# A two-block transformer kernel on one core: four orders changed, and the keys of differential attention prepared as whole tiles, with 64-row matmuls for their low parts

## The chip, the cores and the metric

The kernel is one program on one core of a Trainium2 chip. Five engines take part: TensorE (PE, with its weight loads shown apart as PEld), VectorE (DVE), ScalarE (ACT), GpSimd (POOL) and SyncE (SP), which only issues transfers. The metric is device time in microseconds, median of three executions.

## The reference, cut to what matters

A sequence of 512 tokens of width 1024 in float32 goes through two transformer blocks. The first has sliding-window attention with sinks beside retention, and a convolutional GELU feed-forward. The second has two SwiGLU feed-forwards around a mix of differential attention and a three-branch sparse attention. The part that the larger edit touches is differential attention, with 8 heads, each with two components of 64:

```python
q = apply_rope(q, cos, sin); k = apply_rope(k, cos, sin)
s = jnp.einsum('bqhcd,bkhcd->bhcqk', qb, k).astype(jnp.float32) * scale
s = jnp.where(kpos[None, :] <= qpos[:, None], s, NEG_INF)
p = jax.nn.softmax(s, axis=-1)
a = p[:, :, 0] - lam * p[:, :, 1]
return jnp.einsum('bhqk,bkhe->bqhe', a.astype(v.dtype), v)
```

The other edits lie at the very start (RMS norm of `x`), in the sliding-window attention with its rotary embedding of the retention's queries and keys, and where the compressed branch of the sparse attention hands over to the other two branches.

## The kernel before, in words

**Numbers in two parts.** Every float32 operand of a product is split into a high part (a cast to fp32r) and a low part (the value less its high part), and a product is three matmuls: high by high, high by low, low by high. ScalarE casts, VectorE subtracts. Weights come in chunks of 128x1024 through six slots (`raw`, `Wh`, `Wl`); SyncE reloads a slot once the chunk in it has been used.

**Order.** Nothing schedules the work: each engine runs a program written out by hand, with semaphores between them. What stands behind a waiting instruction on its engine waits too. Softmax tiles are interleaved with steps of matrix products that need nothing new, to fill TensorE's time.

**The start.** SyncE issues `X` tile 0, then the gain `gpre0` (one row broadcast to 128 partitions), `X` tile 1, a weight chunk and so on. `normed(0, 0)` on VectorE needs both `X` tile 0 and the gain. TensorE transposes (`turn_tile`, line 792) and starts the first product (`first_half`, line 739).

**The local attention.** For each of 8 heads, TensorE turns the probabilities (line 963) and multiplies them by the values (lines 985, 986). VectorE does per head `local_low` (`ALl`, 2156), `local_gate` of the next head (`PL`, 2151), `local_max`, `local_sum`, and one `rope_turned` (lines 1943, 2127, 2129), a rotary step of a retention tile, and mostly a weight split (1842).

**Differential attention.** 32 score tiles, `t = 0..31`, four per head; tile `t` has `(t % 4 + 1) * 128` keys and two components `m`, each with its own bank. The queries stand in `Qst` as a stack: for component `m` the 64 partitions of that component hold the high part and the other 64 the low part. `Kh` holds the key's high part in both halves, so that one matmul over 128 rows gives two of the three products (line 854). `Kl` holds the low part in one half and zeros in the other; the matmul of line 855 gives the third product. Line 856 adds the causal mask in bfloat16. GpSimd prepares a head in `qk_low`: it casts the key in two halves (line 574), subtracts in two halves (579) and makes the queries' low halves (585); `v_low` makes the low part of the values `Vst` (592). Each head's other half of `Kh` comes by two transfers of 64 partitions by SyncE (line 490), which waits for the casts (`k_hi`) and stands in the same queue as the weight loads. On TensorE, `values(4h)` waits for the `v_low` of head `h`, and `scores(4h)` for `qk_low` and for the transfers. GpSimd begins head `h` once `high(4(h-2)+2)` has run on ScalarE, which tells it that head `h-2` no longer needs the buffers.

The order of TensorE in the loop is `values(t-2)`, `scores(t+2)`, `turn(t)`, one step of another product.

**The last attention stage.** Before its loop, TensorE does two gate chunks of 8 steps, and `cmp_turn(1)` (line 1159), which needs `cmp_weigh(1)` of VectorE; `unit_turn(0)` (line 1203) then needs the banks that `cmp_low(1)` (`CAl`, line 2370) frees.

Of the kernel before, what the change touches and what calls it, by code (L numbers as in the profile page):

```python
# [7 lines left out]
F32 = mybir.dt.float32  # L8
F32R = mybir.dt.float32r
# [5 lines left out]
P = 128  # L15
# [85 lines left out]
def program(nc, t, out, stop=None):  # L101
# [9 lines left out]
    with ExitStack() as ctx:  # L111
# [111 lines left out]
        Kh = at("Kh", 40, [P, 2, 2, SEQ], F32R)  # L223
        Kl = at("Kl", 80, [P, 2, 2, SEQ], F32R)
        swp_d = at("swp_d", 64, [P, 2, SEQ])
# [101 lines left out]
        st_hi = sem("st_hi")  # L327
        st_zero = sem("st_zero")
        st_lo = sem("st_lo")
        k_twin = sem("k_twin")  # L330
        k_hi = sem("k_hi")
# [55 lines left out]
        def qk_parts(head):  # L387

            return (0, 5)[head] if head < 2 else 5 * head - 1

        def v_parts(head):

            return min(9 + 5 * head, 40) if head else 5

        def q_parts(head):

            return (0, 3)[head] if head < 2 else 3 * head - 1

        def v_casts(head):

            return min(5 + 3 * head, 24) if head else 3

# [44 lines left out]
        def _(sp):  # L447
            w = t["w_all"]
            g = t["g_pre"][0]
            for tt in range(TT):  # L450
                sp.dma_start(X[:, tt, :], t["x"][tt * P:(tt + 1) * P, :]).then_inc(in_x[tt], 16)
                if tt == 0:
                    sp.dma_start(gpre0[:], g.rearrange("(a n) -> a n", a=1).broadcast_to((P, D))).then_inc(in_gain0, 16)
                if tt:
                    sp.dma_start(raw[:, tt - 1, :], w[tt - 1]).then_inc(w_raw[tt - 1], 16)
# [11 lines left out]
            def swaps(m):  # L467
# [15 lines left out]
                if m in TWIN_AT and on("da"):  # L483
                    for head in TWIN_AT[m]:
                        u = head % 2
                        sp.wait_ge(k_hi, 2 * head + 2)
                        for comp in range(2):
                            own = slice(HD * comp, HD * comp + HD)
                            other = slice(HD * (1 - comp), HD * (1 - comp) + HD)
                            sp.dma_start(Kh[other, u, comp, :].bitcast(F32), Kh[own, u, comp, :].bitcast(F32)).then_inc(k_twin, 16)  # L490
                if m == CHUNK0["nsf"] + 3 and on("nsf"):
# [28 lines left out]
        def _(pl):  # L520
# [43 lines left out]
            if on("da"):  # L564
                def qk_low(it, head):

                    u = head % 2
                    k = qkd[:, span(it, 2, 8 + head, 1), :].rearrange("p a n -> p (a n)")
                    if head >= 2:
                        pl.wait_ge(at_hi, 4 * (head - 2) + 3)  # L570
                    for m in range(2):
                        own = slice(HD * m, HD * m + HD)
                        pool.drain()
                        pool.tensor_copy(Kh[own, u, m, :], k[own, :])
                        pool.drain().then_inc(k_hi, 1)
# [20 lines left out]
                pl.wait_ge(roped, 8 + 16)  # L596
                for m in range(2):
                    other = slice(HD * (1 - m), HD * (1 - m) + HD)
                    for u in range(2):
                        last = pool.memset(Kl[other, u, m, :].bitcast(F32), 0.0)  # L600
                last.then_inc(st_zero, 1)
                qk_low(0, 0)
                v_low(0, 0)
                qk_low(0, 1)
                for head in range(2, 8):
# [87 lines left out]
        def _(pe):  # L693
# [149 lines left out]
            def scores(t):  # L843
                i, u, b2 = t % 4, t // 4 % 2, 2 * (t % 2)
                w = width(t)
                q = slice(i * P, (i + 1) * P)
                if i == 0:
                    pe.wait_ge(st_lo, qk_parts(t // 4) + 4)
                    pe.wait_ge(k_twin, 32 * (t // 4) + 32)
                for m in range(2):  # L850
                    b = b2 + m
                    bank_free("da", b, t // 2)
                    dst = ps[b][:, 0:w]
                    tensor.matmul(dst, Qst[:, u, m, q], Kh[:, u, m, 0:w], start=True, stop=False)
                    tensor.matmul(dst, Qst[:, u, m, q], Kl[:, u, m, 0:w], start=False, stop=False)
                    tensor.matmul(ps[b][:, w - P:w], identb[:], causal, start=False, stop=True).then_inc(full[b], 1)
# [245 lines left out]
            if on("da"):  # L1102
                pe.wait_ge(st_zero, 1)
                attention()
# [76 lines left out]
            if on("nsa"):  # L1181
# [80 lines left out]
                gate_steps(1, 0, 4)  # L1262
                gate_steps(1, 4, 8)
                cmp_turn(1)
                for s in range(32):
                    unit_turn(s)
# [49 lines left out]
        def _(ac):  # L1316
# [183 lines left out]
            def nsf_out(c):  # L1500
                chunk_done("nsf", c)
                if c >= 2:
                    ac.wait_ge(st_lo, qk_parts((4, 7)[c - 2]) + 4)
                dst = kcv[:, c, :] if c < 2 else kraw[:, c - 2, :]
                scalar.copy(dst, ps[7][:]).then_inc(free[7], 1)

            def attention():
                exps(0)
                v_high(0)
                exps(1)  # L1510
                qk_high(1)
                for t in range(TOTAL):
# [165 lines left out]
            if on("vda"):  # L1678
                for c in range(7):
                    split(CHUNK0["vda"] + c + LEAD)  # L1680
                    if c == 3 and on("da"):
                        ac.wait_ge(roped, 24)
                        qk_high(0)
                for tt in range(TT):
                    bank_done("vda", tt, 1)
# [70 lines left out]
            if on("nsa"):  # L1756
# [25 lines left out]
                split(CHUNK0["nsa"] + LEAD)  # L1782
                split(CHUNK0["nsa"] + 1 + LEAD)
                unit_exps(1)
                cmp_high(1)
                for s in range(32):
# [48 lines left out]
        def _(ve):  # L1835
# [287 lines left out]
            if on("local"):  # L2123
# [53 lines left out]
                for h in range(8):  # L2177
# [7 lines left out]
                    if h:  # L2185
                        local_sum(h - 1)
                    if h < 7:
                        rope_turned(h + 1)
                    if h < 4:
                        split(CHUNK0["rope_r"] + h + 3 + LEAD)  # L2190
                    if h == 5:
                        split(CHUNK0["rope_r"] + 7 + LEAD)
                local_sum(7)
            if on("vg"):
                splits_t("vg", 5)
# [206 lines left out]
            if on("nsa"):  # L2402
# [38 lines left out]
                cmp_weigh(1)  # L2441
                split(CHUNK0["nsa"] + LEAD)
                split(CHUNK0["nsa"] + 1 + LEAD)
                gate_out(1)
                cmp_low(1)
                for s in range(32):
# [206 lines left out]
```

## Time and profile before

| what | us |
|---|---|
| median of 3 executions (2008.1 to 2018.64) | 2008.75 |
| the profiled execution's own time | 2007.84 |
| its span in the trace | 2006.0 |
| TensorE busy | 1976.0 |
| VectorE busy | 1048.3 |
| ScalarE busy | 810.8 |
| GpSimd busy | 283.2 |

Busy time is the union of an engine's instructions in the span. A matmul's duration includes its way through the array, so that matmuls in a row overlap, and the distance from one start to the next is shorter than the duration.

### The profile page before, as it was taken

What the parts mean: (1) busy time and instruction counts of PE and PEld (TensorE: products, weight loads), DVE (VectorE), ACT (ScalarE), POOL (GpSimd) and SP (SyncE); (2) the same over time, 40 slices, a digit from 0 to 9 for tenths busy, and PEclk for the clock granted to TensorE, in tenths of its full rate; (3) what the DMA queues carried; (4) which work ended last, traced back from release to release, by engine and by line L of the source; (5) the groups of instructions that cost most, each with busy time, mean ns of one, the idle gap of its engine ahead of it and who ended that gap; (6) DMA issues with size and microseconds to landing.
All of it is one profiled execution on the core that took longest, in us unless ns stands there. A gap on an engine that the chain in (4) does not pass through costs nothing.

```text
span 2006.0 us, 25493 instructions
## 1 busy us (share of the span) xinstructions
PE 1976.0 (99%) x10112; PEld 1667.8 (83%) x10112; DVE 1048.3 (52%) x1607; ACT 810.8 (40%) x1474; POOL 283.2 (14%) x290
## 2 busy tenths in 40 slices
PE   7999999999999999999999999999999999999998
PEld 7888888888888888888988788888888888888887
DVE  5766665555353322334563868877775543222333
ACT  5542443333343222233423864466663332222332
POOL 1001000000000000000002734377751000000000
PEclk9999999999999999999999999999999999999999
DMA  6331333333323333332453135221126423333332
GB/s 211 105 95 53 116 106 99 100 95 95 96 94 105 95 96 101 97 95 74 137 153 104 43 115 176 79 64 49 48 64 210 124 67 114 95 99 101 95 95 74
DMA packets 60261, 202.22 MB, mean 101 GB/s; under 512 B 8336, under 2 KB 8368, under 8 KB 59760
## 3 DMA queue, kind: packets, MB, share of 16 engines
q1 hardware_dynamic: 56080, 185.10, 29.9%
q0 software_dynamic: 4064, 15.49, 2.4%
q8 instruction: 81, 1.33, 0.3%
q14 instruction: 36, 0.29, 0.0%
HBM read 181.16 MB, written 8.39 MB: 94 GB/s over the span
## 4 chain that ended last, share of the span: by engine, by line
PE 68%; issue 25%; DVE 3%; ACT 1%; DMA 1%; DVEq 1%; POOLq 1%; POOL 0%; SPq 0%; ACTq 0%
PE ps L700 19%; PE ps L702 19%; PE ps L701 19%; PE ps L1203 2%; PE ps L1192 1%; PE ps L1241 1%; PE ps L1240 1%; PE ps L1193 1%; PE ps L1119 1%; DVE XN L1882 1%; ACT XN L1356 0%; PE ps L1048 0%; PE ps L1194 0%; PE ps L1037 0%; PE ps L792 0%
## 5 line engine op out<-in xcount | busy, mean ns | idle before, releaser
L1842 DVE TENSOR_TENSOR Wl<-raw,Wh 128x1024 fp32r<-128x1024 f32 x307 | 378.5, 1236 | 694.1 <-ACT Wh L1323 692.7
L700 PE MATMUL ps<-HTh,Wh 128*128 128x512 f32 (+1 forms) x1712 | 643.8, 376 | 1.9 <-DVE HTl L2475 1.0
L702 PE MATMUL ps<-HTh,Wl 128*128 128x512 f32 (+1 forms) x1712 | 636.9, 372 | 0.0
L701 PE MATMUL ps<-HTl,Wh 128*128 128x512 f32 (+1 forms) x1712 | 636.6, 372 | 0.0
L1323 ACT CAST Wh<-raw 128x1024 fp32r<-128x1024 f32 x307 | 321.7, 1051 | 741.3 <-DMA raw<-in_w_all 741.3
L700 PEld LDWEIGHTS ps<-HTh,Wh 128*128 128x128 f32 x1712 | 323.1, 189 | 55.9 <-issue 1.8
L702 PEld LDWEIGHTS ps<-HTh,Wl 128*128 128x128 f32 x1712 | 322.4, 188 | 56.3
L701 PEld LDWEIGHTS ps<-HTl,Wh 128*128 128x128 f32 x1712 | 322.8, 189 | 53.2
L700 PE MATMUL ps<-Wh,Yh 128*128 128x512 f32 x528 | 205.8, 390 | 0.0
L702 PE MATMUL ps<-Wh,Yl 128*128 128x512 f32 x528 | 205.5, 389 | 0.0
L701 PE MATMUL ps<-Wl,Yh 128*128 128x512 f32 x528 | 205.4, 389 | 0.0
L656 POOL TENSOR_SCALAR PU<-PU,ugg 128x512 f32<-128x512 f32 (+3 forms) x128 | 139.2, 1103 | 79.3 <-DVE ugg L2414 79.3
L702 PEld LDWEIGHTS ps<-Wh,Yl 128*128 128x128 f32 x528 | 99.1, 188 | 20.7
L700 PEld LDWEIGHTS ps<-Wh,Yh 128*128 128x128 f32 x528 | 99.1, 188 | 20.5
L701 PEld LDWEIGHTS ps<-Wl,Yh 128*128 128x128 f32 x528 | 99.1, 188 | 20.3
L700 PE MATMUL ps<-Wh,HTh 128*128 128x512 f32 (+1 forms) x288 | 110.7, 384 | 0.0
L702 PE MATMUL ps<-Wh,HTl 128*128 128x512 f32 (+1 forms) x288 | 109.4, 380 | 0.0
L701 PE MATMUL ps<-Wl,HTh 128*128 128x512 f32 (+1 forms) x288 | 109.3, 380 | 0.0
L1761 ACT ACTIVATE PU<-ps,umx 128x512 f32<-128x512 f32 (+3 forms) x128 | 65.8, 527 | 53.6 <-DVE umx L2406 53.6
L600 POOL MEMSET Kl<- 64x512 f32 x4 | 2.0, 522 | 453.5 <-DVE qkd L1951 453.5
L702 PEld LDWEIGHTS ps<-Wh,HTl 128*128 128x128 f32 x288 | 54.1, 188 | 10.2
L701 PEld LDWEIGHTS ps<-Wl,HTh 128*128 128x128 f32 x288 | 54.1, 188 | 9.7
(288 smaller groups left out, 2388.0 us busy)
## 6 DMA issues: line engine op xcount, KB each, us to landing
raw<-in_w_all SPq DMA_DIRECT2D x307, 512.0 KB, 3.5
swp_d<-qkd SPq DMA_DIRECT2D x64, 64.0 KB, 2.9
g_dram<-gst SPq DMA_DIRECT2D x16, 256.0 KB, 3.9
ring<-g_dram POOLq DMA_DIRECT2D x16, 256.0 KB, 3.6
X<-in_x SPq DMA_DIRECT2D x4, 512.0 KB, 7.5
swp_r<-qkr SPq DMA_DIRECT2D x16, 128.0 KB, 3.6
gpre<-in_g_pre POOLq DMA_DIRECT2D x4, 512.0 KB, 4.0
Kh<-Kh SPq DMA_DIRECT2D x16, 128.0 KB, 2.3
```

Of the source, the lines that this page charges most:

```text
L656: last = pool.tensor_scalar(p, p, ugg[:, s % 2, i:i + 1], None, ALU.mult)
L700: tensor.matmul(dst, a_hi, b_hi, start=start, stop=False)
L701: tensor.matmul(dst, a_hi, b_lo, start=False, stop=False)
L702: return tensor.matmul(dst, a_lo, b_hi, start=False, stop=stop)
L1119: last = tensor.matmul(ps[kv][:, ht * 64:ht * 64 + 62], cw[:, j, ht * P:(ht + 1) * P], cA[:, kv, j, :], start=j == 0, stop=j == 15)
L1192: tensor.matmul(ps[b][:, o:o + w], q, ksh[:, m, g, 0:w], start=True, stop=False)
L1193: tensor.matmul(ps[b][:, o:o + w], q, ksl[:, m, g, 0:w], start=False, stop=False)
L1203: return tensor.transpose(dst, p[:, a:a + P], ident[:])
L1240: tensor.matmul(ps[b][:, k * P:], v, AUh[:, o:o + w], start=False, stop=False)
L1323: scalar.copy(Wh[:, s, :], raw[:, s, :]).then_inc(w_hi, 1)
L1761: last = scalar.activation(PU[:, (s + 1) % 2, SCORE_AT[i]:SCORE_AT[i] + w], ps[b][:, o:o + w], ACT.Exp, bias=umx[:, s % 2, i:i + 1], accum ...
L1842: vector.tensor_tensor(Wl[:, s, :], raw[:, s, :], Wh[:, s, :], ALU.subtract).then_inc(w_lo, 1)
```

## The change

Five places are changed.

1. SyncE issues `gpre0` behind `X` tile 1 instead of behind `X` tile 0.
2. In the local attention, `rope_turned(6)` and `rope_turned(7)` leave VectorE's iterations 5 and 6 and come behind the loop.
3. Differential attention: `Kl` becomes `Kp`, with the key's high part of both components in plane 0 and the low part in plane 1. GpSimd casts the key in one 128-partition instruction and subtracts in one; the zeroing of `Kl` and its semaphore go. `Kh` is filled by four transfers of 64 partitions per head, each from `Kp`, where two copied within `Kh`. The matmul for the low part of the keys reads only the 64 partitions of its component, from `Qst` and from `Kp`: it is issued with a tile of 64 rows by 128 columns, at row 0 for component 0 and at row 64 for component 1, between matmuls of 128 by 128.
4. The preparation of head 1 moves: GpSimd does `qk_low(0, 1)` ahead of `v_low(0, 0)`, and ScalarE casts head 1's queries within the `vda` product, not after `exps(1)`.
5. At the start of the last attention stage, `cmp_turn(1)` moves ahead of three of the eight steps of the second gate chunk on TensorE, `cmp_high(1)` ahead of `unit_exps(1)` on ScalarE, and `cmp_low(1)` ahead of one weight split and a copy on VectorE.

```diff
             for tt in range(TT):
                 sp.dma_start(X[:, tt, :], t["x"][tt * P:(tt + 1) * P, :]).then_inc(in_x[tt], 16)
-                if tt == 0:
+                if tt == 1:
                     sp.dma_start(gpre0[:], g.rearrange("(a n) -> a n", a=1).broadcast_to((P, D))).then_inc(in_gain0, 16)
...
                         u = head % 2
-                        sp.wait_ge(k_hi, 2 * head + 2)
+                        sp.wait_ge(k_hi, head + 1)
                         for comp in range(2):
                             own = slice(HD * comp, HD * comp + HD)
-                            other = slice(HD * (1 - comp), HD * (1 - comp) + HD)
-                            sp.dma_start(Kh[other, u, comp, :].bitcast(F32), Kh[own, u, comp, :].bitcast(F32)).then_inc(k_twin, 16)
+                            for half in (slice(0, HD), slice(HD, P)):
+                                sp.dma_start(Kh[half, u, comp, :].bitcast(F32), Kp[own, u, 0, :].bitcast(F32)).then_inc(k_twin[u], 16)
...
-                    for m in range(2):
-                        own = slice(HD * m, HD * m + HD)
-                        pool.drain()
-                        pool.tensor_copy(Kh[own, u, m, :], k[own, :])
-                        pool.drain().then_inc(k_hi, 1)
-                    for m in range(2):
-                        own = slice(HD * m, HD * m + HD)
-                        pool.drain()
-                        pool.tensor_tensor(Kl[own, u, m, :], k[own, :], Kh[own, u, m, :], ALU.subtract).then_inc(st_lo, 1)
+                    pool.drain()
+                    pool.tensor_copy(Kp[:, u, 0, :], k)
+                    pool.drain().then_inc(k_hi, 1)
+                    pool.tensor_tensor(Kp[:, u, 1, :], k, Kp[:, u, 0, :], ALU.subtract).then_inc(st_lo, 1)
...
                 if i == 0:
-                    pe.wait_ge(st_lo, qk_parts(t // 4) + 4)
-                    pe.wait_ge(k_twin, 32 * (t // 4) + 32)
+                    pe.wait_ge(st_lo, qk_parts(t // 4) + 3)
+                    pe.wait_ge(k_twin[u], 64 * (t // 8) + 64)
...
                     tensor.matmul(dst, Qst[:, u, m, q], Kh[:, u, m, 0:w], start=True, stop=False)
-                    tensor.matmul(dst, Qst[:, u, m, q], Kl[:, u, m, 0:w], start=False, stop=False)
+                    own = slice(HD * m, HD * m + HD)
+                    tensor.matmul(dst, Qst[own, u, m, q], Kp[own, u, 1, 0:w], start=False, stop=False)
...
-                    if h < 7:
+                    if h < 5:
                         rope_turned(h + 1)
```

The order on three engines, before and now. First GpSimd at the start of differential attention, before; `Kh`, `Kl` and `Qst` are the parts named above, `Vst` the values' low part of a head.

```order
L600 MEMSET Kl 64x512 x4
L574 CAST Kh<-qkd 64x512 x2
L579 TENSOR_TENSOR Kl<-qkd,Kh 64x512 x2
L585 TENSOR_TENSOR Qst<-qkd,Qst 64x512 x2
L592 TENSOR_TENSOR Vst<-vd,Vst 128x512
L574 CAST Kh<-qkd 64x512 x2
L579 TENSOR_TENSOR Kl<-qkd,Kh 64x512 x2
L585 TENSOR_TENSOR Qst<-qkd,Qst 64x512 x2
L574 CAST Kh<-qkd 64x512 x2
```

Now:

```order
L571 CAST Kp<-qkd 128x512
L573 TENSOR_TENSOR Kp<-qkd,Kp 128x512
L579 TENSOR_TENSOR Qst<-qkd,Qst 64x512 x2
L571 CAST Kp<-qkd 128x512
L573 TENSOR_TENSOR Kp<-qkd,Kp 128x512
L579 TENSOR_TENSOR Qst<-qkd,Qst 64x512 x2
L586 TENSOR_TENSOR Vst<-vd,Vst 128x512
L571 CAST Kp<-qkd 128x512
L573 TENSOR_TENSOR Kp<-qkd,Kp 128x512
```

The four memsets are gone, one 128-partition instruction stands where two of 64 did for the cast and for the subtraction, and head 0's values (`Vst`) now stand behind head 1's keys and queries.

VectorE at the end of the local attention, from head 4's `local_sum` (`CATT`), before; `swp_r` and `qkr` are the rotary step, `Wl` a weight split.

```order
L2163 TENSOR_TENSOR CATT<-ps,llo 64x512
L1943 TENSOR_TENSOR swp_r<-swp_r,sin 128x512
L2127 TENSOR_TENSOR qkr<-qkr,cos 128x512
L2129 TENSOR_TENSOR qkr<-qkr,swp_r 128x512
L1842 TENSOR_TENSOR Wl<-raw,Wh 128x1024
L2156 TENSOR_TENSOR ALl<-ps,ALh 128x512
L2158 TENSOR_TENSOR ALl<-ps,ALh 128x384
L2145 TENSOR_TENSOR lsum<-lsum,lsk 128x4
L2147 RECIPROCAL lsum<-lsum 128x4
L2151 TENSOR_SCALAR PL<-PL,lsum 128x128
L2151 TENSOR_SCALAR PL<-PL,lsum 128x256 x3
L2163 TENSOR_TENSOR CATT<-ps,llo 64x512
```

Now:

```order
L2154 TENSOR_TENSOR CATT<-ps,llo 64x512
L1833 TENSOR_TENSOR Wl<-raw,Wh 128x1024
L2147 TENSOR_TENSOR ALl<-ps,ALh 128x512
L2149 TENSOR_TENSOR ALl<-ps,ALh 128x384
L2136 TENSOR_TENSOR lsum<-lsum,lsk 128x4
L2138 RECIPROCAL lsum<-lsum 128x4
L2142 TENSOR_SCALAR PL<-PL,lsum 128x128
L2142 TENSOR_SCALAR PL<-PL,lsum 128x256 x3
L2154 TENSOR_TENSOR CATT<-ps,llo 64x512
L2147 TENSOR_TENSOR ALl<-ps,ALh 128x512
L2149 TENSOR_TENSOR ALl<-ps,ALh 128x384
L2154 TENSOR_TENSOR CATT<-ps,llo 64x512
```

The rotary step no longer stands ahead of the weight split and of head 6's `ALl`, nor that of the next iteration ahead of head 7's; both come behind the last row shown.

VectorE at the start of the last attention stage, from `cmp_weigh(1)`'s last instruction on, before; `CAl` is `cmp_low(1)`, `gst` the gate chunk's copy.

```order
L2365 TENSOR_TENSOR CS_123<-CS_123,cst 128x32x31
L1842 TENSOR_TENSOR Wl<-raw,Wh 128x1024 x2
L2433 COPY gst_132<-ps 128x512
L2370 TENSOR_TENSOR CAl<-ps,CAh 128x512 x2
L2412 RECIPROCAL ugg<-usum 128x4
```

Now:

```order
L2358 TENSOR_TENSOR CS_123<-CS_123,cst 128x32x31
L1833 TENSOR_TENSOR Wl<-raw,Wh 128x1024
L2363 TENSOR_TENSOR CAl<-ps,CAh 128x512 x2
L1833 TENSOR_TENSOR Wl<-raw,Wh 128x1024
L2426 COPY gst_132<-ps 128x512
L2405 RECIPROCAL ugg<-usum 128x4
```

`CAl` now comes behind one split instead of behind two and a copy.

## Rows read from the trace of the kernel before

**Rows 1.** page, part 1: busy us (share of span) and instructions of each engine.
```profile
PE 1976.0 (99%) x10112; PEld 1667.8 (83%) x10112; DVE 1048.3 (52%) x1607; ACT 810.8 (40%) x1474; POOL 283.2 (14%) x290
```

**Rows 2.** stretches: us, busy of PE, PEld, DVE, ACT, POOL, granted clock, DMA share, GB/s.
```profile
1090.00:1195.00 105.00, 97.59 (x670) 81.69 (x670) 83.82 (x200) 77.89 (x226) 59.60 (x52) 1.00 0.26 77
```

**Rows 3.** whom TensorE waited for: us in total, times, longest us.
```profile
PE ps L792 <- DVE XN L1882: 10.1, 4, 7.8
PE ps L700 <- issue: 3.4, 6, 1.0
PE ps L864 <- DVE Pb L2048: 2.2, 5, 0.6
PE ps L854 <- POOL Qst L585: 1.2, 1, 1.2
...
PE ps L985 <- DVE ALl L2156: 1.0, 1, 1.0
...
PE ps L963 <- DVE PL L2151: 0.6, 1, 0.6
```

**Rows 4.** timeline of the start: start us, us, engine, line, op [idle before <-releaser].
```profile
6.41 1.28 DVE L1882 SCALAR_TENSOR_TENSOR XN<-X,rstd,gpre 128x1024 f32<-128x1024 f32 x1 [0.32 <-DMA gpre<-in_g_pre]
...
8.39 1.06 ACT L1356 ACTIVATE XN<-X 128x1024 f32<-128x1024 f32 x1 [2.50 <-DMA X<-in_x]
...
11.52 1.97 PE L792 MATMUL ps<-ident,XN 128*128 128x128 f32 x8 [1.74 <-DVE XN L1882]
```

**Rows 5.** timeline of VectorE at the end of the local attention.
```profile
120.69 0.69 DVE L1943 TENSOR_TENSOR swp_r<-swp_r,sin 128x512 f32<-128x512 f32 x1
...
122.67 1.22 DVE L1842 TENSOR_TENSOR Wl<-raw,Wh 128x1024 fp32r<-128x1024 f32 x1
```

**Rows 6.** timeline of GpSimd, one head of the differential attention.
```profile
1119.85 1.03 POOL L574 CAST Kh<-qkd 64x512 fp32r<-64x512 f32 x1 [0.23 <-issue]
...
1122.57 1.28 POOL L579 TENSOR_TENSOR Kl<-qkd,Kh 64x512 fp32r<-64x512 f32 x1 [0.16 <-issue]
...
1126.90 1.26 POOL L592 TENSOR_TENSOR Vst<-vd,Vst 128x512 fp32r<-128x512 f32 x1 [0.16 <-issue]
```

**Rows 7.** timeline of TensorE at the same place.
```profile
1128.26 0.30 PE L700 MATMUL ps<-Vst,ATdh 128*128 128x128 f32 x1 [1.03 <-issue]
```

**Rows 8.** timeline of VectorE at the start of the last attention stage.
```profile
1281.18 1.19 DVE L2365 TENSOR_TENSOR CS<-CS,cst 128x992 f32<-128x992 f32 x1
...
1286.19 1.29 DVE L2370 TENSOR_TENSOR CAl<-ps,CAh 128x512 fp32r<-128x512 f32 x2 [0.37 <-ACT CAh L1733]
```

**Rows 9.** timeline of TensorE there: second gate chunk, cmp_turn(1), unit_turn(0).
```profile
1279.36 0.47 PE L700 MATMUL ps<-HTh,Wh 128*128 128x512 f32 x1 [0.92 <-DVE gst L2433]
...
1284.93 1.04 PE L1159 MATMUL ps<-ident,CS 128*128 128x128 f32 x8
1287.02 1.38 PE L1203 MATMUL ps<-ident,PU 128*128 128x128 f32 x10 [1.06 <-DVE CAl L2370]
```

**Rows 10.** TensorE groups by shape, 1090 to 1230 us: busy us, mean ns of one.
```profile
L854 PE MATMUL ps<-Kh,Qst 128*128 128x256 f32 x16 | 5.6, 350 | 0.0
...
L855 PE MATMUL ps<-Kl,Qst 128*128 128x256 f32 x16 | 4.5, 280 | 0.0
```

**Rows 11.** timeline of one score tile: weight load, matmul, and the matmul behind it.
```profile
1131.28 0.19 PEld L855 LDWEIGHTS ps<-Kl,Qst 128*128 128x128 f32 x1
...
1131.39 0.28 PE L855 MATMUL ps<-Kl,Qst 128*128 128x256 f32 x1
...
1131.52 0.23 PE L856 MATMUL ps<-band,identb 128*128 128x128 bf16 x1
```

**Rows 12.** timeline of ScalarE, value cast of the same head.
```profile
1125.15 0.62 ACT L1547 CAST Vst<-vd 128x512 fp32r<-128x512 f32 x1
```

**Rows 13.** page, part 6: transfers, count, KB each, us from issue to landing.
```profile
Kh<-Kh SPq DMA_DIRECT2D x16, 128.0 KB, 2.3
```

**Rows 14.** timeline of SyncE: issue of one head's transfers.
```profile
1077.47 1.14 SPq L490 DMA_DIRECT2D Kh<-Kh  x2
```

More of the change, by code:

```diff
@@ L223, in program @@
         Kh = at("Kh", 40, [P, 2, 2, SEQ], F32R)
-        Kl = at("Kl", 80, [P, 2, 2, SEQ], F32R)
+        Kp = at("Kp", 80, [P, 2, 2, SEQ], F32R)
         swp_d = at("swp_d", 64, [P, 2, SEQ])
@@ L327, in program @@
         st_hi = sem("st_hi")
-        st_zero = sem("st_zero")
         st_lo = sem("st_lo")
-        k_twin = sem("k_twin")
+        k_twin = [sem(f"k_twin{u}") for u in range(2)]
         k_hi = sem("k_hi")
@@ L387, in qk_parts @@
         def qk_parts(head):
-            return (0, 5)[head] if head < 2 else 5 * head - 1
+            return (0, 3)[head] if head < 2 else 4 * head - 1
         def v_parts(head):
-            return min(9 + 5 * head, 40) if head else 5
+            return min(7 + 4 * head, 32)
         def q_parts(head):
-            return (0, 3)[head] if head < 2 else 3 * head - 1
+            return (0, 2)[head] if head < 2 else 3 * head - 1
         def v_casts(head):
-            return min(5 + 3 * head, 24) if head else 3
+            return min(5 + 3 * head, 24)
         def nsf_ends(t):
@@ L596, in _ @@
                 pl.wait_ge(roped, 8 + 16)
[L597 to L601, printed above, removed]
                 qk_low(0, 0)
+                qk_low(0, 1)
                 v_low(0, 0)
-                qk_low(0, 1)
                 for head in range(2, 8):
@@ L1102, in _ @@
             if on("da"):
-                pe.wait_ge(st_zero, 1)
                 attention()
@@ L1262, in _ @@
                 gate_steps(1, 0, 4)
-                gate_steps(1, 4, 8)
+                gate_steps(1, 4, 5)
                 cmp_turn(1)
+                gate_steps(1, 5, 8)
                 for s in range(32):
@@ L1502, in nsf_out @@
                 if c >= 2:
-                    ac.wait_ge(st_lo, qk_parts((4, 7)[c - 2]) + 4)
+                    ac.wait_ge(st_lo, qk_parts((4, 7)[c - 2]) + 3)
                 dst = kcv[:, c, :] if c < 2 else kraw[:, c - 2, :]
@@ L1510, in attention @@
                 exps(1)
-                qk_high(1)
                 for t in range(TOTAL):
@@ L1683, in _ @@
                         qk_high(0)
+                    if c == 4 and on("da"):
+                        qk_high(1)
                 for tt in range(TT):
@@ L1783, in _ @@
                 split(CHUNK0["nsa"] + 1 + LEAD)
+                cmp_high(1)
                 unit_exps(1)
-                cmp_high(1)
                 for s in range(32):
@@ L2192, in _ @@
                         split(CHUNK0["rope_r"] + 7 + LEAD)
+                rope_turned(6)
                 local_sum(7)
+                rope_turned(7)
             if on("vg"):
@@ L2442, in _ @@
                 split(CHUNK0["nsa"] + LEAD)
+                cmp_low(1)
                 split(CHUNK0["nsa"] + 1 + LEAD)
                 gate_out(1)
-                cmp_low(1)
                 for s in range(32):
```

## The prediction

> **What bounds the kernel now.** I read the page's busy times first: TensorE is busy for 1976.0 of 2006.0 us [rows 1]. An edit is therefore worth what it takes out of TensorE's 30 us of idle time, less what it adds to TensorE's own work; VectorE at 52% and ScalarE at 40% are idle for half of the span on average, so time on them counts only where TensorE waits for it. Next the list of TensorE's waits [rows 3], which says where the 30 us are: 10.1 at the transposes of the norms, nearly all at the start, where nothing can run yet; 3.4 in six pieces put down to "issue"; 2.2 in five pieces for `Pb`; 1.2 for `Qst`; 1.0 and 0.6 in the local attention. Then the busy time by stretches [rows 2]: of the 105 us from 1090 to 1195, which hold differential attention, TensorE is busy for 97.59, so 7.4 us are idle there. The granted clock is 1.00, the upper level of 2.4 GHz. Last I read timelines of those places, for what ended each wait.
>
> **Edit 1, the gain behind `X` tile 1: 0.** VectorE's first norm began at 6.41, released by the gain; ScalarE's squares of tile 1 began at 8.39, released by `X` [rows 4]. The two transfers are of one size and trade places, so I put the gain at 8.4 and tile 1 at 6.4. Then both norms run back to back, 8.4 + 2 x 1.28 = 11.0, but the first transposes start at 9.8 instead of 7.8 and hold TensorE for about 2 us, as the second set did (1.97, from 11.52) [rows 4]. The second set starts at 9.8 + 1.95 = 11.7 against 11.52. That is 0.2 later, with earlier squares and a first weight cast that may give it back. I take 0, with bounds of 0.6 either way.
>
> **Edit 2, two rotary steps out of the local loop: 1.6 gained.** A step holds VectorE from 120.69 to 122.67, 1.98 us [rows 5]. TensorE then waits 1.0 for `ALl` of head 6 and 0.6 for `PL` of head 7, both behind that step in VectorE's order [rows 3]. With 1.98 gone and 1.6 needed, both waits go, 0.4 to spare; head 7's `ALl` comes 4 us earlier. The steps aren't lost: they run behind the loop, where VectorE has only weight splits, and the retention, which needs them, stands behind the whole `vg` product.
>
> **Edits 3 and 4, differential attention outside the matmuls: 4.0 gained.** The 1.2 us for `Qst` is head 1's preparation, which queues behind head 0's values. It moves ahead of them, and so do ScalarE's casts for it; that wait goes. The six waits of 3.4 us called "issue" I read as waits for GpSimd: `v_low` ran from 1126.90 for 1.26, to 1128.16 [rows 6], and TensorE's first value product of that head started at 1128.26 after 1.03 idle [rows 7]. The other five stand in the same distance to the other heads' `v_low`. Per head the edit takes one cast with its gap (1.03 + 0.23) and one subtraction with its gap (1.28 + 0.16) off GpSimd ahead of `v_low`: 2.7 us [rows 6]. What is late next is ScalarE's cast of the values, 1125.15 + 0.62 = 1125.77 [rows 12], so `v_low` can end at 1125.77 + 1.26 = 1127.03, and TensorE, which was ready at 1128.26 - 1.03 = 1127.23, no longer waits, with 0.1 to spare in this head, the tightest. The five waits for `Pb` (2.2) stay, since they hang on scores that move with TensorE. The sum is 1.2 + 3.4 = 4.6; with so little to spare I take off 0.6. Four transfers replace two: they are 4 x 128 KB per head, each 2.3 us to land [rows 13]. SyncE takes 1.14 to issue two [rows 14], so 2.3 for four, and the last lands 4.6 behind the cast. TensorE's scores of the head stand behind the value product that waits for `v_low`, and `v_low` is the fourth GpSimd instruction of 1.28 behind the cast: 5.1 without gaps. The transfers stay hidden by 0.5 or more. Without that cover, at most the added issue time of 1.14 would show in each of 8 heads, 9 us. The weight loads behind them in SyncE's queue move back by the same 1.14, and TensorE has no wait for a weight in this list [rows 3]. The 4 memsets stood before GpSimd had anything urgent: 0.
>
> **Edit 3, the 64-row matmuls: unknown, taken at 0.** 64 matmuls (32 tiles, two components) change from 128 rows to 64, each between matmuls of 128 rows: 128 changes of shape. No matmul of this trace has 64 rows. From below: a matmul of 256 keys takes 280 ns here [rows 10] with a start-to-start distance of 1131.52 - 1131.39 = 0.13 [rows 11]; the distance goes with the columns, which stay, so I see no gain, and the lower end is 0. The nearest row on a change between neighbours is one of element type: `Kh`'s matmul comes behind the bfloat16 mask or another product and takes 350 ns, `Kl`'s of the same shape behind `Kh`'s takes 280 [rows 10], 70 ns more. At 0.07 for each of 128 changes that is 9 us. From above: at each change the array would empty (0.28 - 0.13 = 0.15) and the weights would be loaded with nothing beside them (0.19) [rows 11]: 0.34 x 128 = 44 us. I take 0: the row of 350 ns also carries the first start after a change of tile and queries, and half of the new changes fall on the very boundary with the mask that pays this already.
>
> The page "TensorE: Matmul & The Clock Gate" of the Trainium skill, section "Why this matters for your kernels", says that one matmul of few rows takes the same time as one of 128; by that the term is 0. No run here shows it yet.
>
> **Edit 5, entry to the last stage: 1.1 gained.** TensorE's second gate chunk ran 1279.36 to 1284.93, 0.70 a step; `cmp_turn(1)` followed, and `unit_turn(0)` began at 1287.02 after 1.06 idle [rows 9], for `CAl`, which ran from 1286.19 [rows 8]. `cmp_turn(1)` moves three steps, 2.1 us, ahead, to 1279.36 + 5 x 0.70 = 1282.86. What it needs was ready at 1281.18 + 1.19 = 1282.37 [rows 8], so it doesn't wait. `CAl` can start near 1284.1 and take 1.29, to 1285.4, before 1285.96, when TensorE is there. `gate_out(1)` moves behind, and only a later gate chunk needs it. 1.1 gained.
>
> **The sum.** 0 + 1.6 + 4.0 + 1.1 = 6.7. The profiled execution took 2007.84, so 2001.1; the median stands 0.9 above that execution, so 2002.0. I add 0.5 for waits that appear in place of those removed: 2002.5.
>
> **The rivals.**
> A, the forecast, 2002.5, by itself 2000 to 2006. For it: every wait it counts has its row and its releaser.
> B, the shape change costs like a change of type. 9 us, less 6.7: 2008.75 - 6.2 + 9 = 2011.5. For it, the 70 ns above; against it, that the columns set the distance elsewhere.
> C, slower: the array empties at each change. At 0.15 the sum is 128 x 0.15 = 19.2, so 2008.75 - 6.2 + 19.2 = 2021.8; with exposed weight loads, 44 us, 2046. It decides from 6.2 / 128 = 48 ns per change upwards, and by over 0.5% from 16.2 / 128 = 127 ns. Against it: no row shows such a thing; for it: 128 places.
> By the page "TensorEngine Tiling (Array Packing)", section "Key Properties", of the Trainium skill, changing the tiling mode drains the TensorE. That is this rival; no row of before can show whether it holds at such a boundary or what it costs.
> D, the differential attention edits don't do what they say: the "issue" waits are not GpSimd's, or ScalarE and VectorE (busy for 83.82 of 105 us there [rows 2]) take their place. Then 1.2 of 4.0 stays, and the time is 2005.3.
>
> **Chances.** A 0.56, B 0.20, C 0.12, D 0.12. Within 0.5% (10 us, about what a measurement of this kernel can tell from no change) is 1998.7 to 2018.8. Faster by more would need more than the 3.4 + 2.2 + 1.2 + 1.0 + 0.6 + 1.1 = 9.5 us of waits behind the start that rows 3 and rows 9 name, so something from the start as well: 0.03, out of A. Slower by more is C and the top of B: 0.13. The rest, 0.84, is no change. The range for 8 in 10 takes in A, B and D: 1999.5 to 2014.
>
> **What would show it.** In the trace after: the waits for `ALl` and `PL` near 124 and 126 are absent; the list has no "issue" waits at the value products and none for `Qst`; `unit_turn(0)` follows without idle time. The start-to-start distance between `Kh`'s matmul, the 64-row one and the mask tells the rest: unchanged (0.13 from the low part's matmul to the mask for 256 keys) means A, longer by 0.05 to 0.1 each B, by 0.15 or more C. A time above 2012 says that the shape change isn't free.

## The result, and the profile after

| | before | after |
|---|---|---|
| median of 12 executions each, us | 2007.62 (2007.0 to 2018.64) | 2021.88 (2012.74 to 2028.9) |
| own time of the profiled execution | 2007.84 | 2023.69 |
| its span | 2006.0 | 2021.8 |

The change makes the kernel slower, by under one per cent: the ratio is 1.0045, 95% interval 1.0028 to 1.0062. The executions of both kernels fall in two groups, about 10 us apart, so the difference depends on what is compared: 14.3 us between the medians, 11.1 between the means, 5.4 between the medians of the two lower groups. Of before, 10 lie at 2007.0 to 2008.8 and 2 at 2018.5 and 2018.6; of after, 3 lie at 2012.74 to 2013.22, 8 at 2021.2 to 2023.7 and one at 2028.9. The two groups are part of the story below, since the change moves most executions from one to the other.

The span grew by 15.8 us. The page's part 1 of after, against [rows 1]: TensorE is busy 21.5 us longer, with the same number of instructions (the stretch at the lower clock, told of below, is part of it), and GpSimd 17 us less.

```profile
PE 1997.5 (99%) x10112; PEld 1680.5 (83%) x10112; DVE 1047.6 (52%) x1607; ACT 810.4 (40%) x1474; POOL 266.1 (13%) x270
```

TensorE's waits, in the form of [rows 3]: engine, tile, line, releaser, then us in total, times, longest.

```profile
PE ps L781 <- DVE XN L1873: 9.9, 3, 9.5
PE ps L1108 <- DMA w2v<-in_w2v: 3.0, 1, 3.0
...
PE ps L1192 <- POOL PU L645: 0.9, 1, 0.9
...
PE ps L854 <- DVE Pb L2039: 0.3, 1, 0.3
```

The waits for `Qst`, for `ALl` and `PL`, for `CAl` and the six "issue" waits are gone, as forecast, and `Pb` (2.2 before) has shrunk to 0.3. The wait of 0.9 for `PU` is new. The one for `w2v`, weights of the sparse attention that the change doesn't touch, has grown to 3.0; the last line of before's list is

```profile
PE ps L1119 <- DMA w2v<-in_w2v: 0.3, 1, 0.3
```

The stretches, in the columns of [rows 2]; the second holds the end of differential attention and the compressed keys of the sparse attention, the third a part of it.

```profile
1090.00:1195.00 105.00, 104.44 (x616) 79.16 (x615) 81.63 (x197) 74.23 (x219) 41.93 (x34) 1.00 0.29 76
1195.00:1262.00 67.00, 64.02 (x370) 58.84 (x370) 39.49 (x50) 24.89 (x40) 20.84 (x24) 0.87 0.48 161
1225.00:1245.00 20.00, 18.76 (x80) 17.78 (x81) 14.30 (x15) 4.39 (x4) 7.49 (x8) 0.57 0.27 74
```

In the first stretch TensorE is busy for 104.44 of 105 us (97.59 before) and yet does less: differential attention, from the first `Kh` matmul to the last value product, took 104.83 us before and takes 113.09. Something makes its matmuls longer. The groups by shape, to be read against [rows 10] (busy us, mean ns of one, idle):

```profile
L845 PE MATMUL ps<-Kp,Qst 64*128 64x256 f32 x16 | 6.1, 380 | 0.0
L843 PE MATMUL ps<-Kh,Qst 128*128 128x256 f32 x16 | 5.6, 350 | 0.0
```

`Kh`'s matmul still takes 350 ns. The low part's, of the same 256 keys, takes 380 where it took 280. The distances from start to start say it more exactly. In the trace before I took a tile of 256 keys [rows 11]; this is one of 384 keys of before, and below it the same of after. Columns: start, us, engine, line, tile.

```profile
1134.28 0.39 PE L854 MATMUL ps<-Kh,Qst 128*128 128x384 f32 x1
1134.51 0.34 PE L855 MATMUL ps<-Kl,Qst 128*128 128x384 f32 x1
1134.68 0.23 PE L856 MATMUL ps<-band,identb 128*128 128x128 bf16 x1
```

```profile
1134.20 0.39 PE L843 MATMUL ps<-Kh,Qst 128*128 128x384 f32 x1
1134.52 0.44 PE L845 MATMUL ps<-Kp,Qst 64*128 64x384 f32 x1
1134.89 0.23 PE L846 MATMUL ps<-band,identb 128*128 128x128 bf16 x1
```

From `Kh`'s matmul to the mask it was 0.40, now 0.69. Over all 64 such places the sum of these distances is 24.17 us before and 41.47 after: 17.3 us for 128 changes of shape, 0.135 each. The two components pay alike. The weight loads show what is lost. The loads of the same places in after:

```profile
1134.14 0.19 PEld L843 LDWEIGHTS ps<-Kh,Qst 128*128 128x128 f32 x1
1134.52 0.18 PEld L845 LDWEIGHTS ps<-Kp,Qst 64*128 64x128 f32 x1 [0.18 <-issue]
1134.89 0.10 PEld L846 LDWEIGHTS ps<-band,identb 128*128 128x128 bf16 x1 [0.18 <-issue]
```

In [rows 11] the low part's load starts at 1131.28 and its matmul at 1131.39: 0.11 of the load ran beside the matmul ahead. Now load and matmul are both put at 1134.52, 0.19 after the load ahead of it has ended (the bracket in the row says 0.18 idle). The median of this lead over the 64 places is 144 ns before and 2 ns after. The load of 64 rows no longer begins beside a matmul of 128 rows. It takes 0.18; the distance from `Kh` to the mask grew by 0.27 per tile and component, a load and 0.09 more. The mask's load led by nothing before either (4 ns, then and now), but the low part's matmul ahead of it now holds its own load: from the low part to the mask the mean distance grew from 163 to 342 ns, from `Kh` to the low part from 214 to 306. So 0.18 of the 0.27 stand at the second boundary and 0.09 at the first.

The second thing stands behind differential attention. TensorE at the first matmul of the compressed keys, before and after:

```profile
1218.30 7.36 PE L1119 MATMUL ps<-cA,cw1k 128*128 128x62 f32 x64 [0.25 <-DMA w2v<-in_w2v]
```

```profile
1226.24 2.18 PE L1108 MATMUL ps<-cA,cw1k 128*128 128x62 f32 x9 [2.98 <-DMA w2v<-in_w2v]
```

The issue of the two transfers concerned, before and after (`w2v` by GpSimd, `cw1v`, 2 MB, by SyncE):

```profile
1212.10 0.53 POOL L526 DMA_DIRECT2D w2v<-in_w2v  x1
...
1212.25 0.33 SPq L471 DMA_DIRECT2D cw1v<-in_cw  x1
```

```profile
1216.15 0.33 SPq L470 DMA_DIRECT2D cw1v<-in_cw  x1
...
1217.30 0.54 POOL L525 DMA_DIRECT2D w2v<-in_w2v  x1
```

Before, GpSimd issued `w2v` 0.15 ahead of SyncE's `cw1v`; after, 1.15 behind it. The list of transfers (count, KB each, us from issue to landing) has GpSimd's two small ones, before and after; `w2k` is issued 0.55 ahead of `w2v`:

```profile
w2k<-in_w2k POOLq DMA_DIRECT2D x1, 128.0 KB, 2.7
w2v<-in_w2v POOLq DMA_DIRECT2D x1, 64.0 KB, 6.2
```

```profile
w2k<-in_w2k POOLq DMA_DIRECT2D x1, 128.0 KB, 7.4
w2v<-in_w2v POOLq DMA_DIRECT2D x1, 64.0 KB, 8.9
```

TensorE reaches the place 5.2 us later than before and `w2v` is issued 5.2 later, so the longer landing, 8.9 against 6.2, is the whole of the added wait: 2.98 against 0.25. Its granted clock falls too: 0.57 on average from 1225 to 1245 (the table of stretches), and in the trace's record it is at the lower of its two levels, 1.2 GHz, for 17.07 us, from 1225.76 on, 0.5 before the wait ends. At half speed that is up to 8.5 us lost beside the wait of 3.0; the 64 matmuls of the compressed keys' first product alone take 13.9 us where they took 7.4. The clock's row of the page's part 2 (40 slices of the span, tenths of full speed) has its one 8 there, and no other dip:

```profile
PEclk9999999999999999999999998999999999999999
```

### The profile page after: what moved, and what is told of

Its sections match the earlier page's. It is cut to its first block, busy times and chain, and to the rows that moved or that the text cites. A ratio compares the mean times of both kernels' runs of the same rounds, so it can differ in the third digit from the quotient of the medians.

```text
span 2021.8 us, 25456 instructions
## 1 busy us (share of the span) xinstructions
PE 1997.5 (99%) x10112; PEld 1680.5 (83%) x10112; DVE 1047.6 (52%) x1607; ACT 810.4 (40%) x1474; POOL 266.1 (13%) x270
## 4 chain that ended last, share of the span: by engine, by line
PE 94%; DVE 2%; DMA 1%; ACT 1%; issue 1%; POOL 1%; DVEq 0%; POOLq 0%; SPq 0%; ACTq 0%
PE ps L689 27%; PE ps L691 27%; PE ps L690 27%; PE ps L1192 2%; PE ps L1108 1%; PE ps L1181 1%; PE ps L845 1%; PE ps L1230 1%; PE ps L1229 1%; PE ps L1182 1%; PE ps L781 1%; POOL PU L645 1%; PE ps L843 1%; DVE XN L1873 1%; PE ps L846 0%
## 5 line engine op out<-in xcount | busy, mean ns | idle before, releaser
L571 POOL CAST Kp<-qkd 128x512 fp32r<-128x512 f32 x8 | 6.7, 840 | 483.9 <-issue 455.4
```

## The experiments

Each was timed in three rounds, with runs of before on the same chip. e1 to e4 share 31 runs of before (median 2008.57; 20 at 2006.8 to 2010.8, 11 at 2015.5 to 2019.7), e5 to e7 and e4b share 28 (median 2008.26; 19 and 9). The two sets ran on different chips, where the lower groups of before have medians of 2007.97 and 2007.55, so a difference taken across the sets carries about 0.4 us. "DA stretch" is the time from the first `Kh` matmul to the last value product in the profile.

**e1_rows128: after, with the low part's matmul over 128 rows.** The other half of the rows now meets a plane that isn't zero, so the scores are other sums.

```diff
-                    own = slice(HD * m, HD * m + HD)
-                    tensor.matmul(dst, Qst[own, u, m, q], Kp[own, u, 1, 0:w], ...)
+                    tensor.matmul(dst, Qst[:, u, m, q], Kp[:, u, 1, 0:w], ...)
```

> The changed kernel, with the low part of the keys multiplied over 128 rows, in one 128x128 matmul as before. Its sums are other ones, since the second plane now holds both components' low parts where zeros stood. Theory (each of 128 changes between 128 and 64 rows costs about 0.14 us): the stretch from the first key score to the last value product falls from 113.1 us to 99 to 102 (before: 104.8, less the 4.6 of waits that went), the distance from the low part's matmul to the mask at 384 keys falls from 0.37 to 0.17, and the total by 11 to 14. Rival (the four transfers and GpSimd's new order slow the stretch): it stays above 109.

Measured: median 2012.46, four runs at 2002.1 to 2003.4 and six at 2012.3 to 2014.6. The total fell by 9.4, less than expected. DA stretch 102.74, above the 99 to 102 of the theory but 10.35 less than after, and the distances from `Kh` to mask add up to 24.08, as before. TensorE's waits:

```profile
PE ps L853 <- DVE Pb L2038: 3.9, 8, 0.5
PE ps L1107 <- DMA w2v<-in_w2v: 2.2, 1, 2.2
PE ps L1191 <- POOL PU L645: 1.0, 1, 1.0
```

The shape is the cause of the longer stretch; the new staging alone doesn't lengthen it. What the stretch gains without it is 104.83 less 102.74 = 2.1, not the 4.0 forecast: the waits for `Pb` grow from 2.2 to 3.9. And the wait for `w2v` is there in this profile too (`w2v` issued 0.8 behind `cw1v`, landed in 8.4, clock at the lower level for 17.07 us): the two groups of runs don't come from the shape.

**e2_before_rows64: before, with nothing but the low part's matmul over 64 rows.** `Kl`'s other half is zero, so the sums stay.

```diff
-                    tensor.matmul(dst, Qst[:, u, m, q], Kl[:, u, m, 0:w], ...)
+                    own = slice(HD * m, HD * m + HD)
+                    tensor.matmul(dst, Qst[own, u, m, q], Kl[own, u, m, 0:w], ...)
```

> The kernel before, with nothing changed but the low part's matmul, over its own 64 rows. Theory (0.14 us per change of rows): the stretch grows from 104.8 us by 18 less what TensorE's waits there absorb (up to 7), so to 116 to 123, and the total to 2018 to 2026. Rival (the matmul is free, the rest of the edit slows the stretch): 104.8 and 2007.6, as before.

Measured: median 2024.34, four runs at 2014.6 to 2018.3, six at 2024 to 2027.8; ratio 1.0051 (1.0026 to 1.0075). The distances add up to 41.46, the DA stretch is 113.14, below the 116 to 123 of the theory. The same 17.3 us, alone: 113.14 - 104.83 = 8.3 of them stay as time, since before had waits there which the longer matmuls cover (`Qst`, "issue" and `Pb`, 6.8 us in [rows 3], of which 0.2 is left in this profile); that accounts for 6.6 of the 9.0 that don't show, and the rest is not assigned. The wait for `w2v` is there too (`w2k` issued at the same time as `cw1v`, at 1219.25, `w2v` 0.55 behind, landed in 8.2; clock at the lower level for 13.65 us):

```profile
PE ps L1120 <- DMA w2v<-in_w2v: 2.0, 1, 2.0
...
PE ps L700 <- issue: 0.2, 1, 0.2
```

**e3_after_w2_early: after, with `w2k` and `w2v` issued ahead of `inputs(0)` on GpSimd**, eight additions with their own waits.

```diff
-                inputs(0)
                 load(w2k[:], t["w2k"], in_cw)
                 load(w2v[:], t["w2v"], in_cw)
+                inputs(0)
                 inputs(1)
```

> The changed kernel, with GpSimd issuing the two loads w2k and w2v ahead of its first eight additions (inputs(0)) and so 8 us ahead of the 2 MB load cw1v of SyncE. Theory (w2v queued behind cw1v, TensorE waited 3.0 us, and its clock then fell to the lower level for 17 us): no wait at the compressed branch's first product, granted clock 1.00 from 1195 to 1262, every run near 2012.5. Rival (the clock falls because of the sparser matmuls of differential attention, or for a reason outside the kernel): the clock still falls, and most runs are at 2021 to 2023.

Measured: median 2012.61 (2011.62 to 2015.87), one group of runs. Ratio to before 1.0 (0.9981 to 1.0019); before's upper group is in that ratio, and e3 lies 4.6 us above the median of its lower group. GpSimd issues `w2v` at 1205.72, SyncE `cw1v` at 1217.86, and the wait and the fall of the clock are both gone:

```profile
1195.00:1262.00 67.00, 67.00 (x420) 60.62 (x420) 52.34 (x65) 28.58 (x44) 23.39 (x24) 1.00 0.56 186
1225.00:1245.00 20.00, 20.00 (x156) 19.02 (x156) 17.98 (x21) 7.47 (x10) 4.47 (x6) 1.00 0.46 127
```

`w2k` and `w2v` land 3.7 and 4.1 after their issue. One run of the ten, 2015.87, has a mean granted clock of 0.996 where the others have 0.998 or 0.999, so a fall of the clock isn't excluded in every execution. In the profiled one the wait of 3.0 and the lower clock went together, and in the medians both cost 2021.88 - 2012.61 = 9.3 us. What is left of after is the shape, less what the other edits gain.

**e4_before_w2_late: before, with the two loads held back on GpSimd** until the result of differential attention has been written out.

```diff
                 inputs(0)
+                pl.wait_ge(yd_out, 16 * TT)
+                pl.wait_ge(da_sq, 2)
+                pool.drain()
                 load(w2k[:], t["w2k"], in_cw)
```

> The kernel before, with GpSimd waiting, ahead of its loads w2k and w2v, for what SyncE waits for ahead of cw1v, so that w2v is issued some 0.6 us behind cw1v where it stood 0.15 ahead. Theory (the order of these two transfers decides): TensorE waits 2 to 4 us for w2v, its granted clock falls to 0.5 behind that, and the total is 2016 to 2020 in every run, as in the odd run of before at 2018.6. Rival (the order is of no account): the wait stays under 1.5 us, no fall of the clock, 2007 to 2009.

Measured: median 2018.85, nine runs at 2015.9 to 2020.6 and one at 2009.23; ratio 1.0036 (1.0016 to 1.0055). `w2v` is issued at 1214.23, 1.1 behind `cw1v` (1213.12), and before now shows what after shows:

```profile
PE ps L1122 <- DMA w2v<-in_w2v: 2.4, 1, 2.4
```

```profile
1195.00:1262.00 67.00, 64.63 (x360) 58.66 (x359) 42.50 (x55) 25.96 (x40) 21.27 (x24) 0.87 0.44 147
1225.00:1245.00 20.00, 20.00 (x97) 18.61 (x97) 10.40 (x12) 5.58 (x8) 4.91 (x7) 0.65 0.17 52
```

`w2k` and `w2v` land 7.0 and 7.7 after their issue, against 2.7 and 6.2. Not all of the wait is the order: `w2v` is issued 2.1 later than in before while TensorE gets there 1.6 later, which gives 0.6 of the 2.1 added, and the longer landing gives 1.5. This execution also has two short falls of the clock that before's lacks (3.41 us each, from 126.11 and from 1105.74), which lengthen its DA stretch to 106.08 and aren't explained. Between before's lower group and the median of e4 lie 10.9 us.

The landing times sort all ten profiles. Where GpSimd issued `w2k` ahead of `cw1v` by 0.7 us or more (before, e3, e4b, e5, e6, e7), `w2k` landed in 2.7 to 3.7 and `w2v` in 3.5 to 6.2. Where it was at the same time or behind (after, e1, e2, e4), they took 6.7 to 7.4 and 7.7 to 8.9.

**e4b_before_w2_early: before, with the edit of e3.**

```diff
-                inputs(0)
                 load(w2k[:], t["w2k"], in_cw)
                 load(w2v[:], t["w2v"], in_cw)
+                inputs(0)
                 inputs(1)
```

> The kernel before with GpSimd's loads w2k and w2v ahead of its first additions. Theory (the runs of before at 2015 to 2020, 13 of 43, are those in which w2v lost its 0.15 us lead over cw1v): no run above 2012, the rest at 2007. Rival (they come from something outside this pair of transfers): about a third of the runs stay at 2015 to 2020.

Measured: median 2006.98 (2005.95 to 2007.73), no run in the upper group; ratio 0.998 (0.9962 to 0.9997). Before's own runs near 2018 (22 of the 71 told of here) fit the same race, lost in a third of its executions; none of them was profiled, so that the order was reversed in them is inferred from their absence here. With the race out of both kernels, the change costs 2012.61 - 2006.98 = 5.6 us, across the two sets.

**e5_pairs: e3, with the two components' matmuls side by side** (`Kh`, `Kh`, low, low, mask, mask), which makes 64 changes of 128. This is not the only thing that it changes: the two banks of a tile are complete later, and together.

```diff
-                for m in range(2):
-                    ... Kh[m]; low[m]; mask[m]
+                for m in range(2):
+                    ... Kh[m]
+                for m in range(2):
+                    ... low[m]
+                for m in range(2):
+                    ... mask[m]
```

> The changed kernel with w2k and w2v loaded early, and the six matmuls of a score tile in another order: both matmuls of the high part, then both 64-row ones (rows 0 to 63, then 64 to 127), then both masks. Theory (the cost is per change of tile shape, not per 64-row matmul): changes fall from 128 to 64, so the distances from first to last matmul of the score tiles fall by about 8.6 us in sum, the stretch of differential attention from 113.1 to 103 to 106, and the total from 2012.6 to 2002 to 2005. If in addition the two 64-row matmuls, which sit on different rows, run beside each other, up to 4 us less. Rival (the cost belongs to each 64-row matmul, whatever its neighbours): 113 and 2012.6.

Measured: median 2006.92 (2005.18 to 2009.18); ratio 0.9976 (0.9957 to 0.9996); DA stretch 109.2. Both the median and the stretch lie outside the theory's 2002 to 2005 and 103 to 106. The median is 5.7 below e3, where taking all changes out brings 10.9 (e6).

The trace shows more than a price per change. A tile of 384 keys, two matmuls to a row (start, us, then as above):

```profile
1135.00 0.57 PE L842 MATMUL ps<-Kh,Qst 128*128 128x384 f32 x2
1135.49 0.44 PE L845 MATMUL ps<-Kp,Qst 64*128 64x384 f32 x2
1135.87 0.29 PE L848 MATMUL ps<-band,identb 128*128 128x128 bf16 x2
```

The two 64-row matmuls, on rows 0 to 63 and 64 to 127, take 0.44 together, as one of them took in after: the second starts 2.5 to 4 ns behind the first (medians for the four widths), and they run side by side. The distance from them to the mask is as in e3 (0.37 at 384 keys in both), so that boundary costs what it cost. From the first `Kh` matmul of a tile to its last mask, the 32 tiles add up to 28.1 us, against 42.7 in e3 and 25.3 in e1: 14.6 less than e3, where the theory had 8.6 for the changes. Only 2.7 of the 17.3 are left, so the rival by which each 64-row matmul has its own price, whatever its neighbours, is out. The stretch doesn't show it, because the waits for `Pb` grow from 0.3 to 6.5 and the profiled execution has 6.83 us at the lower clock, about 3.4 lost:

```profile
PE ps L856 <- DVE Pb L2041: 6.5, 12, 0.9
```

```profile
1130.00:1135.00 5.00, 5.00 (x25) 4.26 (x24) 2.86 (x8) 2.89 (x8) 2.99 (x3) 0.54 0.46 107
```

**e6_rows128_zero: e3 with the low part over 128 rows and correct sums.** GpSimd still casts a head's key in one instruction, but the low part is subtracted in two halves into `Kl`, whose other halves are zeroed once, and the matmul is that of before.

```diff
-                    pool.tensor_copy(Kp[:, u, 0, :], k)
+                    pool.tensor_copy(Kp[:, u, :], k)
                     pool.drain().then_inc(k_hi, 1)
-                    pool.tensor_tensor(Kp[:, u, 1, :], k, Kp[:, u, 0, :], ALU.subtract).then_inc(st_lo, 1)
+                    for m in range(2):
+                        own = slice(HD * m, HD * m + HD)
+                        pool.tensor_tensor(Kl[own, u, m, :], k[own, :], Kp[own, u, :], ALU.subtract).then_inc(st_lo, 1)
...
-                    tensor.matmul(dst, Qst[own, u, m, q], Kp[own, u, 1, 0:w], ...)
+                    tensor.matmul(dst, Qst[:, u, m, q], Kl[:, u, m, 0:w], ...)
```

> The changed kernel with w2k and w2v loaded early, and with the low part over 128 rows of a tile whose other half is zero, as the kernel before has it: the key is still cast as one tile and spread by four transfers, the subtraction goes back to two halves. Theory: differential attention 102.5 to 103.5 us as with 128 rows before, no fall of the clock, total 2002 to 2003, faster than the kernel before by 5 us. Rival (the halves for the subtraction bring GpSimd's lateness back): 104.8 and 2004.5.

Measured: median 2001.73 (2000.92 to 2002.3), one group; ratio 0.9941 (0.9922 to 0.9961). DA stretch 102.76. The 64-row shape thus costs 2012.61 - 2001.73 = 10.9 us across the two sets; within one set, the lower group of e1 (median 2003.0) gives 9.6, and the DA stretches give 10.4. All the rest of the change gains 2006.98 - 2001.73 = 5.3.

**e7_entry: e6, with `unit_exps(1)` ahead of a weight split on ScalarE and `unit_gate(1)` ahead of `cmp_low(1)` on VectorE.** In e3's trace `ugg`, which GpSimd's `PU` needs, came behind `CAl`, a split and a copy, so that GpSimd began 1.77 behind `unit_turn(0)`, against 0.87 before.

```diff
                 split(CHUNK0["nsa"] + LEAD)
-                split(CHUNK0["nsa"] + 1 + LEAD)
-                cmp_high(1)
                 unit_exps(1)
+                split(CHUNK0["nsa"] + 1 + LEAD)
+                cmp_high(1)
...
+                unit_gate(1)
                 cmp_low(1)
```

> The previous kernel of this call with the entry to the last attention stage in another order: ScalarE does unit_exps(1) ahead of the second weight cast, VectorE unit_gate(1) ahead of cmp_low(1). Theory (TensorE's 0.9 us for PU at its third unit came from gate and exponentials put back behind the second split, so that GpSimd's multiplication began 1.77 us behind unit_turn(0) instead of 0.87): that wait is gone, 1.0 us less than the previous kernel, 2001 to 2002. Rival (GpSimd's chain of 4.3 us sets that place by itself): the same time as the previous kernel.

Measured: median 2000.83 (2000.44 to 2001.29); ratio 0.9949 (0.993 to 0.9969). That is 0.9 below e6, and the two ranges overlap by 0.4. The wait for `PU` is gone: the third unit's turn starts at 1293.04 against 1294.05. The list has one of 0.9 for a weight's low part (`Wl`) instead, but it lies at 19.0, in the first product, which this edit doesn't touch:

```profile
PE ps L862 <- DVE Pb L2048: 3.9, 8, 0.5
...
PE ps L698 <- DVE Wl L1842: 0.9, 1, 0.9
```

It is the fastest version here, 7.4 us below the median of before and 6.2 below e4b.

## Why the prediction was wrong

The forecast was 2002.5 with a range to 2014; the median is 2021.88. Step by step:

- **The start, 0: right.** The first turn of the local attention comes at 70.52 against 71.33 before, but before's order gives 70.31 and 71.08 in e4 and e2, and after's 70.75 in e3. The four profiles with before's order lie at 70.31 to 71.79, the six with after's at 70.34 to 70.84: at most 0.5 gained on average, within the scatter.
- **The local attention, 1.6: right, a little low.** From its first turn to its last value product it took 59.76 and takes 57.53: 2.2 gained, and both waits are gone.
- **Differential attention outside the matmuls, 4.0: right in kind, half in size.** The waits for `Qst` and for "issue" went but for one of 0.2, as forecast; e1 and e6 show 2.1. The step "The five waits for `Pb` (2.2) stay" failed: with 128 rows (e1, e6) they became eight, of 3.9. As I read it, TensorE reaches the probabilities earlier, and what makes them has become no faster; no run tests that. The 0.6 that I took off for new waits was too little: they took 1.7, and 6.8 us of waits became 4.1.
- **The 64-row matmuls, 0: the step that failed.** I took 0 because the number of columns stays and because "half of the new changes fall on the very boundary with the mask that pays this already". Neither held. The columns set the distance only while the next load runs beside the matmul ahead, and rows 11 showed how much of the load was hidden (0.11 of 0.19); the boundary with the mask grew most, by 0.18 of the 0.27. The matmul itself is longer too, 380 ns for 256 keys against 280. The price is 0.135 us a change, 17.3 in all, inside my bounds of 0 and 44 and near rival C's 0.15. With the measured 10.4 us in this place my sum would have given 2012.9. In time it is less, 8.3 us in the old order (e2) and 10.35 in the new (after against e1), since longer matmuls cover waits; the waits that the other edits removed can't be covered once more.
- **The rule on tiling.** "TensorEngine Tiling (Array Packing)", section "Key Properties", of the Trainium skill, says that changing the tiling mode drains TensorE. The traces of after, e1 and e2 agree that such a change costs time, 0.135 us each; that the array empties there they don't show, only that the 64-row load and its matmul start together. I gave it a chance of 0.12; as the page that speaks of two unlike neighbours it should have weighed more than the one that speaks of a single matmul's time, whose rule didn't hold at these boundaries (280 against 380 ns).
- **The entry to the last stage, 1.1: right, and given back.** From the compressed keys to `unit_turn(0)` it is 1.26 shorter in e3 than before, and `unit_turn(0)` follows without idle time; then the wait of 0.9 for `PU`, which I had not named, takes most of it back; 0.3 stays. e7 removes it.
- **Missing altogether: the race of two transfers and the clock behind it, 9.3 us.** Differential attention ended 5.2 later in span time, and GpSimd and SyncE issued their loads later, but not by the same amount: `w2v` by 5.2 (1212.10 to 1217.30), `cw1v` by 3.9 (1212.25 to 1216.15). I had only looked for waits that a move within differential attention could raise, and wrote that TensorE had no wait for a weight; before's full list has one, the 0.3 for `w2v`, and one of its three executions stood at 2018.64. That rival C's number, 2021.8, is the median measured is chance: C is right that each change has a price, and with that and the other edits the time is 2012.6 (e3). The median is this plus 9.3.

The sum of the terms as measured: -2.2 - 2.1 + 10.35 - 0.3 = +5.8, against 5.6 between e4b and e3; with the race, +15.1, against 14.3 between the medians. The start is left at 0 in it, though e3's profile is 0.6 earlier there than before's.

What stays open: why `w2k` and `w2v` land so much later when they are issued with or behind a transfer of 2 MB. The ten profiles show that landing goes with the order of issue, and e3 and e4b that the wait and the upper group go when the two loads come 12 us ahead, which changes both the order and the slack; how the queues share the engines none of them shows. Nor is it shown why the clock stays low for 13.65 to 17.07 us after a wait of 2.0 to 3.0, or why e4 and e5 have short falls elsewhere. The one run of after at 2028.9 isn't explained.

## What to carry to other kernels

Cutting the rows of a matmul that stands alone between matmuls of 128 saved nothing here and cost 0.27 us each, of which 0.18 is its weight load, which no longer runs beside its neighbour; a half of zeros was cheaper (e6). If 64-row matmuls are used, those on the two halves of the rows belong next to each other, where they ran side by side (e5). Give any change that shifts a stage by some microseconds a second look at the loads behind it: whether a small one is issued just ahead of a large one on another queue or just behind it can decide whether TensorE waits. And price a wait of 3 us on a busy TensorE not at 3 us, but with the stretch at the lower clock that can follow it.

## What the runs showed of the hardware that was not expected

- A change between a matmul of 128 rows and one of 64 costs 0.135 us (128 changes, 17.3 us, the same in two kernels); the load of the 64-row weights starts with its matmul (lead 2 ns) where that of 128-row weights leads it by 144 ns.
- Around a wait of TensorE of 2.0 to 3.0 us for `w2v`, its granted clock fell from 2.4 to 1.2 GHz: for 17.07 us in after (wait 2.98), e4 (2.37) and e1 (2.16), for 13.65 in e2 (1.98). The fall came between 0.5 us before the end of the wait and 1.9 after it. Before's wait of 0.25 at the same place was followed by no fall.
- Two 64-row matmuls on the two halves of the rows, next to each other, start 2.5 to 4 ns apart and take 0.44 us together at 384 keys (e5).
- A transfer of 128 KB issued 0.7 us ahead of one of 2 MB on another queue landed in 2.7 us, issued 0.6 us behind it in 7.4.
- One kernel can have two groups of times 10 us apart, and moving two small loads changes how many runs fall in the upper one: 9 of 28 and 11 of 31 runs of before, 0 of 10 in e4b, 9 of 10 in e4.
